# Differential attention on one Trainium2 core: near bias of every second softmax added by the vector engine

## What is computed

```python
def probs(qb, k):                       # group A, called with (q1, k1) and (q2, k2)
    s = einsum('bqhd,bkhd->bhqk', qb, k) * scale + bias
    s = where(allowed, s, -inf)         # key chunk <= query chunk, chunks of 64
    return softmax(s)
p = probs(qb1, k1) - lam * probs(qb2, k2)
out = einsum('bhqk,bkhd->bqhd', p, v)
```

## Time and profile before

| | us |
|---|---|
| median of 3 runs | 741.91 (740.95 to 744.52) |
| the profiled execution | 741.63 |
| its span, first to last instruction | 739.8 |

### The profile page before, as it was taken

How to read it: one execution, slowest core, us unless ns; L and a number is a source line. 1 busy time by engine, 2 the same in 40 slices (tenths; PEclk the granted TensorE clock), 3 DMA queues, 4 the chain that set the end, 5 groups by cost and what they waited for, 6 DMA issues and landing times.

```text
span 739.8 us, 12056 instructions
## 1 busy us (share of the span) xinstructions
PE 720.9 (97%) x4184; PEld 602.1 (81%) x4184; DVE 615.8 (83%) x1293; ACT 322.6 (44%) x723; POOL 366.1 (49%) x445
## 2 busy tenths in 40 slices
PE   8999999999999999999999999999899999999996
PEld 7757888888888898999888888888787878788886
DVE  5678999999997979898599999999689898646554
ACT  7547131131313666667531131314777767522222
POOL 5220222223556859771135555547999999612210
PEclk9999999999999999999999999999999999999999
DMA  7340211212220010113021112220010112312231
GB/s 282 113 143 20 57 44 44 57 43 57 68 62 1 1 43 2 43 31 100 16 70 44 47 39 57 53 76 1 30 44 10 50 46 89 127 57 95 78 113 58
DMA packets 24564, 44.58 MB, mean 60 GB/s; under 512 B 3076, under 2 KB 10936, under 8 KB 24376
## 3 DMA queue, kind: packets, MB, share of 16 engines
q1 hardware_dynamic: 23336, 42.76, 19.5%
q10 hardware_dynamic: 1168, 1.05, 0.4%
HBM read 35.40 MB, written 6.57 MB: 57 GB/s over the span
## 4 chain that ended last, share of the span: by engine, by line
PE 85%; DVE 5%; POOL 4%; issue 2%; DMA 2%; ACT 1%; SPq 0%; POOLq 0%; DVEq 0%; ACTq 0%
PE psum L1273 41%; PE psum L1494 12%; PE psum L1356 5%; PE psum L1368 4%; PE psum L1334 4%; PE psum L1337 4%; PE psum L1383 3%; PE psum L1228 3%; PE psum L1211 3%; PE psum L1193 2%; PE psum L1165 2%; DMA xs<-in_x 1%; PE psum L1341 1%; PE psum L1340 1%; DVE probs L1761 1%
## 5 line engine op out<-in xcount | busy, mean ns | idle before, releaser
L609 POOL TENSOR_TENSOR w_lo<-w_raw,w_hi 128x512 fp32r<-128x512 f32 x60 | 77.5, 1294 | 215.5 <-ACT w_hi L807 215.2
L1640 DVE MATCH_REPLACE8 score<-top,score 128x640 f32<-128x640 f32 (+5 forms) x176 | 157.4, 906 | 0.0
L1635 DVE MAX8 top<-score 128x8 f32<-128x640 f32 (+5 forms) x176 | 148.7, 910 | 1.1
L807 ACT ACTIVATE w_hi<-w_raw 128x512 fp32r<-128x512 f32 x60 | 37.4, 629 | 209.8 <-PE psum L1273 206.8
L983 ACT ACTIVATE probs<-psum,small 128x384 f32<-128x384 f32 (+7 forms) x128 | 94.8, 741 | 38.4 <-DVE small L1700 30.0
L1273 PE MATMUL psum<-big_hi,w_hi 128*128 128x512 f32 x256 | 99.7, 389 | 0.0
L1273 PE MATMUL psum<-big_hi,w_lo 128*128 128x512 f32 x256 | 99.6, 389 | 0.0
L1273 PE MATMUL psum<-big_lo,w_hi 128*128 128x512 f32 x256 | 99.6, 389 | 0.0
L1273 PE MATMUL psum<-w_hi,big_hi 128*128 128x512 f32 x192 | 74.7, 389 | 0.0
L1273 PE MATMUL psum<-w_lo,big_hi 128*128 128x512 f32 x192 | 74.7, 389 | 0.0
L1273 PE MATMUL psum<-w_hi,big_lo 128*128 128x512 f32 x192 | 74.7, 389 | 0.0
(11 more groups left out here) (195 smaller groups left out, 1630.7 us busy)
## 6 DMA issues: line engine op xcount, KB each, us to landing
w_raw<-in_w_in SPq DMA_DIRECT2D x62, 256.0 KB, 2.6
xs<-in_x SPq DMA_DIRECT2D x8, 512.0 KB, 7.0
k_high_twice<-k_high_twice SPq DMA_DIRECT2D x16, 256.0 KB, 3.7
xres<-in_x SPq DMA_DIRECT2D x8, 512.0 KB, 4.3
out_y<-y_out SPq DMA_DIRECT2D x8, 384.0 KB, 2.9
w_tail<-in_w_out SPq DMA_DIRECT2D x10, 256.0 KB, 2.6
bias_scratch<-bias_row SPq DMA_DIRECT2D x1, 2304.0 KB
bias<-bias_scratch SPq DMA_DIRECT2D x12, 128.0 KB, 3.0
```

What stands on the lines that cost most here:

```text
L609: pool.tensor_tensor(lo[:, 0:cols], w_staged(n)[:, 0:cols], hi[:, 0:cols].bitcast(f32), ALU.subtract).then_inc(w_lo_made, 1)
L807: act.activation(w_parts(n)[0][:, 0:cols], w_staged(n)[:, 0:cols], ACT.Copy).then_inc(w_hi_made, 1)
L1635: ins = dve.max(top8[:, i - SEL0, :], sc)
L1640: ins = dve.match_replace(sc, top8[:, i - SEL0, :], sc, TAKEN)
```

## The change

In the first attention, the unit m = 1 of each step no longer gets its bias from the two identity passes on PE. `near_high` is loaded with an unsplit, masked copy of the bias of heads 0 to 2 at the start and with that of head 3 later on, and DVE adds it with `soften`: the far part gets a minimum (L1700's instruction on fewer columns), then the near part gets bias and minimum in one instruction. In both attentions the near part of a row longer than 256 columns is now 224 columns (`BAND - SAME`): the first 32 of the 256 lie wholly in the bucket whose bias is zero. In the second attention POOL's `near` makes 224 columns, `far_min` takes 32 more columns and `soften` 32 fewer.

```diff
+SAME = 32
+        def near_width(i):
+            return P * (i + 1) if i < SEL0 else BAND - SAME
...
+            def keep_bias(h):
+                sp.dma_start(near_high[:, h % 3, :],
+                             bass.AP(scratch, h * RELS + P - 1, [[nh * RELS - 1, P], [1, BAND]])
+                             ).then_inc(bias_kept[h // 3], 16)
...
             for h in range(A_HEADS):
                 load_bias(h)
+            for h in range(3):
+                keep_bias(h)
...
             copy_keys(0, 2)
+            sp.wait_ge(max_ready, 2 * TILES)
+            keep_bias(3)
             load_chunk(Q0 + 3)
...
-                pool.tensor_tensor(near_slot(k), bias[:, A_HEADS + 2 * b + m, :], mask[:, end - BAND:end], ALU.add
-                                   ).then_inc(near_made, 1)
+                pool.tensor_tensor(near_slot(k)[:, SAME:BAND], bias[:, A_HEADS + 2 * b + m, SAME:BAND],
+                                   mask[:, end - BAND + SAME:end], ALU.add).then_inc(near_made, 1)
...
-                    near = max(c, length - BAND)
-                    banded = ph == 0 and near < c + w
+                    near = max(c, length - near_width(i))
+                    banded = ph == 0 and m == 0 and near < c + w
...
+            dve.wait_ge(bias_kept[0], 16 * 3)
+            link(dve.memset(near_high[0:CHUNK, :, BAND - CHUNK:BAND], MASKED))
...
-                if ph == 0:
+                if ph == 0 and m == 0:
                     dve.tensor_reduce(negmax[:, u % 4:u % 4 + 1], score_of(u, 0, P * (i + 1)), AX.X, ALU.min
                                       ).then_inc(max_ready, 1)
+                elif far and ph == 0:
+                    far_done[u] = later(dve.tensor_reduce(farmin[:, u % 4:u % 4 + 1], score_of(u, 0, far), AX.X,
+                                                          ALU.min))
...
-                added = bias[:, h, BAND - w:BAND]
+                added = near_high[:, b % 3, :] if ph == 0 else bias[:, A_HEADS + 2 * b + m, :]
+                added = added[:, BAND - w:BAND]
...
             far_min(0, 0, 0)
             far_min(0, 0, 1)
+            soften(0, 0, 1)
             for s in range(STEPS):
...
                 combine(s)
+                if s == 3 * TILES - 2:
+                    dve.wait_ge(bias_kept[1], 16)
+                    link(dve.memset(near_high[0:CHUNK, 0, BAND - CHUNK:BAND], MASKED))
                 if s + 1 < STEPS:
                     far_min(0, s + 1, 1)
+                    soften(0, s + 1, 1)
```

More of the change, by code:

```diff
@@ L218, in build @@
         bias_masked = sem("bias_masked")
+        bias_kept = [sem("bias_kept"), sem("bias_kept_last")]
         biasA_split = sem("biasA_split")
@@ L1695, in far_min @@
                 i = place_of(ph, s)[1]
-                far = P * (i + 1) - min(BAND, P * (i + 1))
+                far = P * (i + 1) - near_width(i)
                 u = (ph * STEPS + s) * 2 + m
                 dve.wait_ge(s_ready, u + 1)
-                if ph == 0:
+                if ph == 0 and m == 0:
                     dve.tensor_reduce(negmax[:, u % 4:u % 4 + 1], score_of(u, 0, P * (i + 1)), AX.X, ALU.min
                                       ).then_inc(max_ready, 1)
+                elif far and ph == 0:
+                    far_done[u] = later(dve.tensor_reduce(farmin[:, u % 4:u % 4 + 1], score_of(u, 0, far), AX.X,
+                                                          ALU.min))
                 elif far:
@@ L1712, in soften @@
                 length = P * (i + 1)
-                w = min(BAND, length)
+                w = near_width(i)
                 u = (ph * STEPS + s) * 2 + m
-                h = b if ph == 0 else A_HEADS + 2 * b + m
                 least = UNSEEN_MIN
@@ L1726, in soften @@
                     dve.wait_ge(near_made, k + 1)
-                    added = near_slot(k)
+                    added = near_slot(k)[:, SAME:BAND]
                 dve.tensor_tensor_reduce(out=o, in0=o, in1=added, scale=1.0,
```

## The result

| | before | after |
|---|---|---|
| median of 5 runs, us | 741.91 (740.95 to 744.52) | 737.99 (737.92 to 738.03) |
| ratio | | 0.9944 (0.9925 to 0.9964) |
| profiled execution, us | 741.63 | 737.92 |
| its span, us | 739.8 | 736.1 |

The account below looks back on a forecast made before the run. PE was taken as the bound (busy 97%), with DVE also at its limit in the long steps of the first three blocks. 741.6 - 1.0 (first attention) - 0.9 (second attention) = 739.7 us, range 733.8 to 743.5.

Parts of the forecast that it names:

- DVE's price per unit: First attention, m = 1 minimum split into two DVE instructions: 1.39 against 1.13 us, +0.26 us per unit, 24 units.
- rival 2: First attention, blocks 0 to 2: POOL's instructions hold DVE's near pass (L1728), giving 746.7 us; chance 0.07.
- rival 3: PE's new gaps let its clock fall: two drops of some 1.5 us each, giving 742.7 us; chance 0.06.
- The edits costed at nothing: Three more loads on SP's queue, `keep_bias(3)`'s wait, two DVE memsets and `soften`'s wait: all hidden, no time added.
- Block 2, +1.1 forecast: First attention, third block: DVE's +1.6 us up to PE's last hold at 327.63, PE's -0.5 behind it, net +1.1.
- shift it by what DVE got up to there: Each block's last place where DVE or ACT held PE moves later by DVE's added work before it, +1.6 in block 2.
- Block 1, +0.2 forecast: First attention, second block: DVE's +1.2 us up to PE's last hold at 288.50, PE's -1.0 behind it, net +0.2.
- Block 0, -0.5 forecast: First attention, first block: +0.66 us up to PE's last hold at 252.68, PE's -1.2 behind it, net -0.5.
- Block 3, -1.8 forecast: First attention, last block: PE alone sets the pace and sheds 2.1 us, less 0.3 given back, net -1.8.
- The allowance of 0.3: First attention, block 3: 0.3 us given back for long steps where DVE is closest to PE; ends 0 and 1.0.
- that wait goes; past it PE is bound by its own queue: Second attention: POOL 2.8 us sooner removes PE's 0.87 us wait for head 3's keys, -0.9; bounds 0 and -1.5.
- rival 1: First attention: buffers even out more than assumed, giving 732.8 us at the extreme, typically 733 to 736.5; chance 0.27.

Follow-up runs that it names:

- e2: Changed kernel with the second attention's near part back at 256 columns, so only the first attention's change remains: 741.59 us, ratio 0.9986.
- e9: The changed kernel run once more, on the same chip as e10 and e11, as their reference: 738.12 us, ratio 0.9940.
- e3: Kernel before, with the m = 1 identity passes of the first attention left out and nothing in their place: 739.73 us, ratio 0.9964.
- e4: Changed first attention with PE's m = 1 identity passes kept too (bias counted twice), second attention as before: 743.14 us, ratio 1.0003.
- e5: Kernel before, with POOL's splits for heads 2 and 3 of the first attention cut from 512 to 32 columns: 741.14 us, ratio 0.9989.
- e7: Changed kernel with POOL's first three output-weight split pairs moved behind the split of head 3's keys: 737.07 us, ratio 0.9933.
- e10: e7 plus the m = 0 near bias moved to DVE on head 3's tiles 5, 3, 1 and 0: 736.24 us, ratio 0.9918.
- e11: e7 plus the m = 0 near bias moved to DVE on all eight tiles of head 3: 736.78 us, ratio 0.9917.

## Where the prediction held and where it failed

**Held.**
- *DVE's price per unit.* 0.26 us forecast; 1.38 against 1.13 measured.
- *No delay of the near pass by POOL (rival 2).* 458 to 461 ns beside POOL. What POOL holds is `factor` and `combine`, as before.
- *No drop of the clock in the first attention (rival 3).* 1.00 in all four blocks.
- *The edits costed at nothing.* Projections and output stage are unchanged within 0.1 us.

**Right sum, wrong terms.** The first attention was forecast at -1.0 us and measured at -1.2 (e2 -1.2, e9 -1.1). That is luck: block 2 came out 1.0 us better than its term, blocks 0 and 3 together some 0.9 worse (by the table, whose block 3 lacks a step), and the term that came out right, block 1's, was added up from two that didn't.
- *Block 2, +1.1 forecast, +0.11 measured (e2 +0.12).* The step that failed is "shift it by what DVE got up to there": it took DVE's time at the last hold as rigid. `factor` and `combine` take 12.9 us in that block and some 8.3 by the durations of block 3; the difference, 4.6 us, is waits for POOL, and 1.5 of the 1.6 us went into them. PE's -0.5 there didn't come either (e3: -0.18).
- *Block 1, +0.2 forecast, +0.13 measured.* The number is right, the working isn't: neither did DVE's +1.2 arrive (e4: +0.32) nor PE's -1.0 (e3: -0.19).
- *Block 0, -0.5 forecast, -0.22 measured.* e3 gives -0.84 for PE's part where the working had -1.2.
- *Block 3, -1.8 forecast for eight steps; seven gave -1.21, and the stretch of the earlier trace rows, 30.40 long, is 28.90 now.* Two terms were too large. The first is PE's price. In e3, where DVE has no new work, the seven steps shed 1.35 us with 16 matmuls fewer, 0.08 each where the working had 0.11 and 0.12. By steps it is 0.23 to 0.26 in four of them, with two wide matmuls gone in each, but 0.10 in the first, which loses four narrow ones over two banks, 0.16 in the second and 0.12 in the last, with two narrow ones. The durations of the chain, taken one by one, overstate what leaves with them. The second is DVE: after is 0.14 behind e3; the step from 344.45 to 349.07 alone is 4.62 long against 4.43 in e3. The allowance of 0.3 was twice too large.

The Trainium skill ("TensorE: Matmul & The Clock Gate", Back-to-back issue gap) was weighed in the prediction: 6.6 us for all removed matmuls where the rows gave 8.3. The seven steps of block 3 lost 10 wide and 6 narrow ones; by the page's figures that is an estimated 10 x 0.109 + 6 x 0.056 = 1.4 us, by the chain's rows 10 x 0.12 + 6 x 0.11 = 1.9. The page gives these as the gap of single matmuls taken alone; the measured 1.35 agrees with them in sum, and by terms in the wide ones. The chain's rows misled for the narrow matmuls alone: in e3 the five steps that lost two wide ones each gave 1.13 us, 0.11 per matmul, and the two steps that lost the six narrow ones 0.22, 0.04 each, where the rows had 0.66.

**Mis-sized.** *The second attention: -0.9 forecast with bounds 0 and -1.5, measured -2.1, outside of them.* The failing step is "that wait goes; past it PE is bound by its own queue". The 0.87 us of the earlier trace rows were read as all that POOL's chain costs. They were what was left of it after PE had itself been held up: it was 1.3 us later than in e3 behind a `shares` copy that waited for a POOL instruction. Where PE arrives hangs on the ends of POOL's instructions as well: it came 2.0 us sooner in after (85.2 against 87.2), the keys 1.9 sooner, and the wait stayed at 0.9. The clock drop of the earlier trace rows, which the prediction used for the first attention alone, is one of two ways into that delay; e5 came to it without a drop. The saving per instruction, 0.08, was too high as well (0.06): 2.8 us forecast for the chain, 2.1 measured; all of that 2.1 counted.

**The marks that the prediction named.** 36 matmuls on each line: yes. Near pass at 0.46: yes. DVE over 28.5 us in block 1: no, 27.48. Waits for ACT of 2 us a block: half of it, over blocks 0 to 3 together 3.3 us, where before had 1.2 (us in total, times, longest):

```profile
PE psum L1349 <- ACT probs L998: 3.3, 6, 0.9
```

Block 3 at 28.6: 28.90. No wait for the keys at head 3: it is there as before, 0.9. And rival 1, that the buffers even out more, was right against my numbers in block 2 (+0.1 measured, +1.1 forecast) but far off in size, since it had -2.1 and -1.6 in blocks 1 and 2: DVE's slack was largely in the waits for POOL (and in block 0 in 5.3 us without work, where the prediction says 3 to 4), and so was PE's gain.

## What to carry to other kernels

Busy time of an engine can contain waiting for another. Before adding work to it, compare its shortest instruction with the same one where the other engine is still (here 531 against 220 ns), and see whether its long instances end with an instruction of the other. Added work may be taken from that difference first (1.5 of 1.6 us in block 2, 0.9 in block 1, 0.3 in block 0), and work taken from a third engine may give little until the waiting ends. A wait in a trace is what is left when the waiting engine was late itself: before calling it the most that a faster producer can give, look for what delayed the waiter, and whether the producer did that too. One trace doesn't settle which delay it was; here the fallen clock looked like it, and runs with the same late arrival without it said otherwise. Take the worth of a removed matmul from a stretch with and without it, not from its share in the chain.

## Unexpected in the hardware

- A DVE instruction of 128 x 1 with operands in SBUF took 220 ns beside a still POOL and 531 on average over a block beside a busy one (348 in another block); with work put ahead of it, 381 (253). All 14 held instances in before ended within 0.02 us of the end of a POOL instruction.
- A DVE copy with one input in SBUF (`shares`, 128 x 128) was held as well: 0.23 us at the least, up to 1.3, and all 30 instances over 0.3 us in before ended 0.08 or 0.09 us behind a POOL instruction.
- At the start of the second attention PE has nothing to do for 1.7 us, and in six of thirteen profiled executions the granted clock then fell to 1.2 GHz for some 3.4 us, in seven it didn't, in kernels with the same code there too. The stage was 0.75 us longer with the drop where PE set the end (e7 against e10 and e11) and no longer where POOL did.
- POOL's sum of two fp32 tiles lost 60 ns for 32 of 256 columns, 1.9 ns a column, where its mean duration over its columns would say 2.6.
